# A margin between inputs and place in a planner's order, and the gate constants moved behind the first norm

## What is computed

```python
h = concat(meta, x)                                   # (T, 1024)
u = rmsnorm(h, g1)
q, f, i, og, xp, ga, gb = split(u @ w_in)             # 4x1024, 512, 2x1024 columns
# branch A: gated linear recurrence, 8 heads of 128x128 state
S_t = diag(f_t) S_{t-1} + (1 - f_t) i_t^T ; o_t = S_t^T silu(q_t)    # f_t = lb + (1-lb) sigmoid(f)
ya = (rmsnorm_per_head(o) * sigmoid(og)) @ w_br_hgrn
# branch B: trailing means over 2, 4, 8, 16 tokens less the token, a linear map per group
yb = pool_mixer(xp) @ w_br_pool
h = h + (sigmoid(ga) * ya + sigmoid(gb) * yb) @ w_out
u = rmsnorm(h, g2)
h = h + (silu(u @ w_gate) * (u @ w_up)) @ w_down      # 2816 wide
return rmsnorm(h, g3)[16:]
```

## Time and profile before

| | us |
|---|---|
| median of 3 runs | 2253.82 (2252.72 to 2254.36) |
| profiled execution, its time | 2258.92 |
| its span, slowest core (others 2246.5 to 2254.9) | 2257.1 |
| PE busy / idle in that span | 2117.0 / 140.1 |
| ACT, DVE, POOL busy | 980.1, 997.2, 644.8 |

### The profile page before, as it was taken

The page is one execution under the profiler, slowest core; times in us unless marked ns, Lnnn a source line. Parts: engine busy times, 40 slices in busy tenths (PEclk is TensorE's granted clock), DMA queues, the critical chain, the costliest instruction groups (busy, mean ns, idle before and its releaser), DMA issues.

```text
span 2257.1 us, 38090 instructions; the slowest of 8 cores (2246.5 to 2257.1 us)
## 1 busy us (share of the span) xinstructions
PE 2117.0 (94%) x11476; PEld 1103.3 (49%) x11476; DVE 997.2 (44%) x1752; ACT 980.1 (43%) x1470; POOL 644.8 (29%) x816
## 2 busy tenths in 40 slices
PE   5777999999999999999999999999999999999997
PEld 2333555555455544544455445544554445444446
DVE  4442564476446322653374224744453225632223
ACT  4642773574467212752484125731761127532111
POOL 4342231130322142153412412246022521422200
PEclk9879999999999999999999999999999999999999
DMA  9999899898744667448445585466445584475576
GB/s 178 225 186 241 183 225 234 179 213 210 218 146 135 175 183 208 143 133 246 134 136 155 174 234 160 122 190 196 148 129 157 170 230 140 131 209 162 158 197 187
DMA packets 223093, 405.24 MB, mean 180 GB/s; under 512 B 24208, under 2 KB 64528, under 8 KB 222896
## 3 DMA queue, kind: packets, MB, share of 16 engines
q1 hardware_dynamic: 189200, 328.30, 51.2%
q0 software_dynamic: 32064, 72.63, 16.0%
q10 hardware_dynamic: 1632, 1.88, 0.3%
HBM read 385.94 MB, written 53.08 MB: 195 GB/s over the span
## 4 chain that ended last, share of the span: by engine, by line
PE 72%; DVE 7%; DMA 6%; issue 6%; ACT 5%; POOL 3%; DVEq 0%; ACTq 0%; POOLq 0%; SPq 0%
PE psa L477 62%; PE psa L641 5%; DMA wr<-wpk 4%; DMA fa<-xT 2%; DVE ba L612 2%; POOL fa L570 1%; PE psa L759 1%; DVE fa L742 1%; DVE ba L784 1%; DVE fa L780 1%; ACT fa L740 1%; ACT fa L733 1%; POOL fa L574 1%; POOL ba L574 1%; ACT fa L744 1%
## 5 line engine op out<-in xcount | busy, mean ns | idle before, releaser
L477 PE MATMUL psa<-ba,wr 128*128 128x456 bf16 (+2 forms) x9536 | 1889.8, 355 | 23.1 <-DVE fa L670 8.3
L477 PEld LDWEIGHTS psa<-ba,wr 128*128 128x128 bf16 x9536 | 924.1, 98 | 897.0 <-issue 51.8
L882 ACT ACTIVATE fa<-psa 128x456 f32<-128x456 f32 (+1 forms) x198 | 108.4, 551 | 352.3 <-PE psa L477 327.3
L883 DVE TENSOR_TENSOR ba<-psa,fa 128x456 bf16<-128x456 f32 (+1 forms) x198 | 123.8, 631 | 301.4 <-PE psa L477 259.9
L570 POOL TENSOR_TENSOR fa<-fa 128x456 f32<-128x456 f32 (+1 forms) x160 | 156.2, 983 | 320.2 <-DMA fa<-xT 185.7
L750 POOL TENSOR_TENSOR ba<-fa 128x456 bf16<-128x456 f32 (+1 forms) x48 | 56.0, 1167 | 502.2 <-ACT fa L733 210.3
L641 PE MATMUL psa<-wr,ba 128*114 128x512 bf16 (+1 forms) x576 | 135.4, 388 | 10.3 <-DMA wr<-wpk 5.7
L344 POOL DMA_DIRECT2D wr<-wpk x145 | 77.1, 532 | 216.7 <-PE psa L477 101.4
L780 DVE SCALAR_TENSOR_TENSOR fa<-fa,psa 128x128 f32<-128x128 f32 x288 | 97.7, 339 | 70.5 <-PE psa L773 64.9
L742 DVE TENSOR_TENSOR_SCAN fa<-ba,fa 128x456 f32<-128x456 bf16 (+1 forms) x72 | 80.6, 1119 | 102.2 <-ACT fa L740 101.1
L843 POOL TENSOR_TENSOR ba<-fa 128x456 bf16<-128x456 f32 (+1 forms) x48 | 56.1, 1169 | 242.7 <-DVE fa L840 242.7
(11 more groups left out here) (84 smaller groups left out, 1653.9 us busy)
## 6 DMA issues: line engine op xcount, KB each, us to landing
wr<-wsc SPq DMA_DIRECT2D x1040, 256.0 KB, 2.9
wr<-wpk POOLq DMA_DIRECT2D x128, 256.0 KB, 12.4
wsc<-wr POOLq DMA_DIRECT2D x128, 256.0 KB, 13.4
wr<-wsc SPq DMA_DIRECT2D x72, 192.0 KB, 2.6
fa<-xT SPq DMA_DIRECT2D x6, 1824.0 KB, 14.9
outT<-fa SPq DMA_DIRECT2D x6, 1824.0 KB, 10.7
wr<-wsc SPq DMA_DIRECT2D x72, 128.0 KB, 2.4
fa<-xT SPq DMA_DIRECT2D x2, 1840.0 KB, 14.1
```

The costliest lines, as they stand in the source:

```text
L477: last = e.matmul(ps[bank][:, 0:c1 - c0], lhsT=sl[0].ap(i * 128, (i + 1) * 128), rhs=s_.ap(c0, c1), start=(start and i == 0), stop=(stop a ...
L882: yield act(lambda e: e.activation(out=sg.ap(0, nt), in_=ps[bg][:, 0:nt], func=AF.Silu), [PS(bg)], [sg.rg(0, nt)], tset="S", banks=[bg])
L883: yield dve(lambda e: e.tensor_tensor(out=ACT[fc].ap(0, nt), in0=ps[bu][:, 0:nt], in1=sg.ap(0, nt), op=ALU.mult), [PS(bu), sg.rg(0, nt)], ...
```

## The change

`MARGIN` is added to the ready time of each candidate before it is compared: 1.0 us on PE, 0.3 us on ACT, DVE and POOL, nothing on SP. A candidate whose inputs are ready earlier than the engine's free time less the margin has the same `t` as before. `emit` is unchanged: neither the modelled start of an emitted operation nor its waits contain the margin. The second edit moves the call of `consts()` behind the eight applications of the opening norm. No operation is added or removed.

```diff
+MARGIN = {"pe": 1.0, "act": 0.3, "dve": 0.3, "pool": 0.3, "sp": 0.0}
@@ in run()
                     rec_eng = "dma" if op.dma else op.eng
-                    t = P.ready(rec_eng, rr, op.w)
+                    t = P.ready(rec_eng, rr, op.w) + MARGIN[op.eng]
                     if op.eng == "sp" and op.hold and t > P.free["sp"] + 1.0:
                         held.append((t, s))
                         continue
@@ in norm()
-            if mode == "split" and t == 0:
-                consts()
             if apply_gate:
                 yield apply_gate
             for kc in range(8):
                 yield dve(lambda e, kc=kc: e.scalar_tensor_tensor(out=dst[kc].ap(c0, c1), in0=src[kc].ap(c0, c1), scalar=PRM.ap(gcol + kc, gcol + kc + 1),
...
                           flags=[(out_flag, t, kc, c0)] if out_flag else [])
+            if mode == "split" and t == 0:
+                consts()
```

## The result

The changed kernel takes 2197.16 us (median of 4 runs, 2196.77 to 2198.17) against 2254.09 us; the ratio is 0.9748, 95% interval 0.9731 to 0.9764. It is 57 us faster, where 14 were forecast. In some executions one die shows a lower granted clock and takes some per cent longer; all ratios compare executions without that.

The account below looks back on a forecast made before the run. PE's 2117 us of busy time was taken as the bound, with 140 us idle movable, after a weight-starved opening. Terms -20 - 5 - 2 - 3 + 0 + 3 + 13 = -14 us took 2253.8 to 2240 us; range 2225 to 2265.

Parts of the forecast that it names:

- the boundary waits: PE's 3 to 5 us waits for DVE at tile boundaries, 14.6 us in all: 2 us taken as gain.
- The likeliest case: Whole kernel: the holes close and little is lost, 2240 us, own range 2227 to 2249; chance 0.55.
- signs of being wrong: Busy PE changing over 5 us, head spacing staying 9.5, weight waits (264 to 530) above 25, bare L612 waits above 30.
- The floor: PE's busy time over the whole span: 2117 us can't shrink unless matmuls are removed; only 140 us of idle can move.
- The DMA term: Tiles 1 and 2: longer heads draw first-time FFN units forward where DMA is saturated; +13 us for both.
- Case C: Tiles 1 and 2: drawn-forward FFN units wait for DMA, 2273 us; decides from 2 extra first-time units a head; chance 0.17.
- The norm's matmul: L582 behind the norms, waiting 10.8 us in 12 for POOL's sums: 5 us taken as gain.
- the head's waits: Waits of L759, L773 and L792 behind 264, 24.2 us in all: 20 us taken as gain.
- the constants: Opening norm: applications start 1.85 us earlier, but PE's chain of waits runs through weight transfers; 0 taken.
- the groups in front of L759 and L773: In a head's timeline, two groups of eight L477 matmuls would stand before each of these lines.
- case D: Between tiles: longer heads exhaust the FFN reserve and norm 2 lies bare in several tiles; 2272 us, chance 0.11.
- The head's cycle: Spacing of heads in the body: grows by 3.6 us from 9.5 to about 13.1 us.

Follow-up runs that it names:

- slack 1.5: Kernel before with a margin of 1.0 us on PE alone and PE's slack raised from 0.5 to 1.5 us: ratio 1.0069.
- slack 1.0: Kernel before, no margin, with PE's slack raised from 0.5 to 1.0 us: two times, 2281.8 and 2274.1 us, no ratio.

## Why the prediction was wrong

The mechanism was right: fresh inputs give way, the holes close, FFN work fills them, the opening and the boundary waits stay. The likeliest case gave 2240 us, its range 2227 to 2249 and the whole range 2225 to 2265; measured 2197. One of the prediction's own signs of being wrong came true: PE's busy time changed by over 5 us. Four terms of the sum were off, all on one side.

**The floor.** "2117 us is a floor unless matmuls are removed" is the step that failed most. Busy time fell by 19.6 us. Two things are in it. A group of eight takes 1.71 us as a record but follows the last one by 1.55: the end of the last matmul is counted, 0.16 us, and it lies under the next group only if there is no hole. (The ends of matmuls are modelled in the profile; the starts are not.) From 1129.42 to 1131.40 are 1.98 us for a group of 1.55: the hole cost 0.43 us, not the 0.27 in the bracket. Behind the opening the waits in the list fell from 91 to 14, 77 x 0.16 = 12 us. The rest is in good part the clock: by the granted clock in the traces, PE was busy at 1.2 GHz for 55.8 us before and for 47.7 us after, and half of the difference, 4.1 us, is work done at the slower rate. Long holes cost here as well: behind the one of 4.07 us at 1097.33 the eight matmuls of L641 take 3.63 us, where eight take 1.89 at full clock. Counted over the whole span, PE's busy time falls into 142 pieces before and 72 after. Over the thirteen kernels (all but the one with the longer latency), busy time, less half of that at 1.2 GHz, grows by 0.20 us with each piece, and none lies over 1.7 us off that line. By it the 70 pieces are 14 us, and with the 4.1 us of the clock 18 of the 19.6 us have a cause. Busy time went broadly with the span: 2093.2 us at 2182.4, 2100.2 at 2205.6 (PE's margin alone), 2123.3 at 2278.0 (slack 1.5), 2126.1 at 2280.2 (slack 1.0).

**The DMA term**, +13 us, was 0. Tile 1's heads show no wait for weights, where 5 to 20 us were forecast. The mechanism exists: with 2.0 us it showed, with 9.7 us of waits for weights. Its size at 1.0 us was wrong, because I took the growth of a head of tile 5, from 9.5 us by 3.6, and put 2.5 first-time units in it. Tile 1's heads were already 10.1 us long and grew by 2.1 us, 1.4 groups. Issues of first-time loads from 264 to 350, before and after:

```profile
wr<-wpk POOLq DMA_DIRECT2D x26, 256.0 KB, 11.8
```

```profile
wr<-wpk POOLq DMA_DIRECT2D x30, 256.0 KB, 12.9
```

Four loads more in 86 us, where I had put twenty for the eight heads. Case C's point of decision (2 units more a head) was not reached at 1.0 us and was passed at 2.0, where a head of tile 1 grew by 6 us; the waits came from 382 on, behind the first and ahead of the second place that C named.

**The norm's matmul** (L582): taken 5 of 10.8 us, measured 10.1. The mean wait of 0.9 us lay under the margin, and the row with its longest of 2.6 led me to halve it. I also took it for a number of the kernel, and it is one of the slowest core: the least waited 4.0 us.

**Waits that I left out**, since they had no large row: those of L600, and of L759, L477 and L641 with other releasers. They were 9.3 of 58.9 us in the list of the earlier trace rows and are 1.1 now.

Right were: the head's waits (taken 20 of 24.2, measured 21.7), the boundary waits in their size (taken 2, measured 0.4), the constants (0, measured 1.0001), the groups in front of L759 and L773, and the reserve (case D): no bare wait for want of work, even with heads of 15.4 us in tiles 3 to 8. The reason given for the boundary waits holds in part: the longest left, 5.1 us, and the one of 2.7 at 2047.12 stand behind applications of 0.61 to 0.69 us each, which do not overrun, and with 2.0 us from tile 3 on only the latter is left. L795's waits (2.1 us of 5.3) stayed just above the third that was forecast. The head's cycle I put at 13.1 and it is 11.3 (tile 5) to 12.2: L795 stays behind three groups. For tile 0 I took 3 us and there is nothing: its idle time is 71.5 against 71.8. The other margins were put at +3 and gain 14 us alone, some 2 beside PE's, within the intervals nothing.

By the medians the forecast missed by 43 us; by the span, where the profiled execution of the kernel before lay 5 us above its median, by 48: 19.6 of busy time, 13 of DMA, 5.1 of the norm's matmul, 8.2 of waits left out, 3 of the other margins, less about 1 for the rest. And the measured side adds up: -21.7 - 10.1 - 0.4 - 8.2 = -40.4 us of listed waits, 1.9 us of shorter ones and the opening, and -19.6 us of busy time make the 61.9.

## What to carry to other kernels

In a list scheduler for engines that run in order, look at slack less margin: a preference for an operation that isn't ready yet plans a hole, and in an in-order queue an error of the model can make one more. Give the bottleneck engine's operations a reserve, as long as there is filler; where the filler itself is short of something (here first-time weights), use less. How much is to be measured: here 1.0 us gained 2.5%, 2.0 us behind tile 2 gained 3.4%, and 1.5 us there no more than 1.0. Look at the waits and not at the ratio alone, since a new order brings long waits of its own. And price a hole on TensorE by the distance between starts, not by the idle time in front of an instruction.

## What the runs showed of the hardware

PE's busy time isn't a constant of the work: the same 11476 matmuls were busy for 2093.2 to 2126.1 us (the kernel with the longer latency left out). A group of eight with 456 columns costs 1.55 us between others and 1.71 before a hole. A DMA share is not a rate: from 455 to 530 the kernel before moved 227 GB/s at a share of 0.99, the changed one (second row) 241 GB/s at 0.87, with PE never idle. The mix was another, 16 converting first-time loads against 8, so this doesn't show that the former could have moved more of the same:

```profile
455.00:530.00 75.00, 73.68 (x451) 40.17 (x451) 55.59 (x114) 53.53 (x81) 20.34 (x38) 1.00 0.99 227
```

```profile
455.00:530.00 75.00, 75.00 (x442) 40.89 (x441) 45.84 (x89) 48.91 (x73) 11.84 (x22) 1.00 0.87 241
```
